# Expert weights fetched four K-rows at a time instead of two, in the same ring of twelve

## The reference, cut to what matters

```
gate = min(h @ w_gate[e] + b_gate[e], 7)
up   = clip(h @ w_up[e] + b_up[e], -7, 7)
y    = ((up + 1) * gate * sigmoid(1.702 * gate)) @ w_down[e] + b_down[e]
```

## Time and profile before

| | |
|---|---|
| median of 3 runs | 1600.43 us (1598.94 to 1605.11) |
| the profiled execution | 1595.97 us |
| its span, first to last instruction | 1594.2 us |
| PE busy | 1525.1 us (96% of the span) |
| DVE busy | 1325.8 us (83%) |
| ACT busy | 1086.6 us (68%) |
| moved by DMA | 464.81 MB, 292 GB/s over the span |
| mean granted TensorE clock | 0.984 of full |

### The profile page before, as it was taken

How to read it: one execution, slowest core, us unless ns; L and a number is a source line. 1 busy time by engine, 2 the same in 40 slices (tenths; PEclk the granted TensorE clock), 3 DMA queues, 4 the chain that set the end, 5 groups by cost and what they waited for, 6 DMA issues and landing times.

```text
span 1594.2 us, 29429 instructions
## 1 busy us (share of the span) xinstructions
PE 1525.1 (96%) x10445; PEld 1262.4 (79%) x10445; DVE 1325.8 (83%) x1458; ACT 1086.6 (68%) x1309; POOL 585.3 (37%) x366
## 2 busy tenths in 40 slices
PE   7999987889999999999999999999999999999993
PEld 6877777886878888878888888888888888888872
DVE  4256455555689999999999999999999999999994
ACT  4245431103468887788888888888878888888881
POOL 7000312101022233344445554544554544545532
PEclk9999999999999999999999999999999999999997
DMA  8321110001399999999999999999999999999974
GB/s 295 91 67 40 40 41 3 4 4 67 134 407 383 389 385 375 390 367 396 381 376 395 394 392 391 391 368 385 393 392 396 385 379 384 389 392 398 384 291 129
DMA packets 81414, 464.81 MB, mean 292 GB/s; under 512 B 11658, under 2 KB 12870, under 8 KB 33216
## 3 DMA queue, kind: packets, MB, share of 16 engines
q1 hardware_dynamic: 71424, 438.68, 69.6%
q0 software_dynamic: 9248, 25.05, 7.1%
q10 hardware_dynamic: 672, 0.07, 0.0%
HBM read 449.16 MB, written 23.66 MB: 297 GB/s over the span
## 4 chain that ended last, share of the span: by engine, by line
PE 86%; DVE 9%; DMA 2%; issue 1%; ACT 1%; DVEq 0%; POOLq 0%; POOL 0%; ACTq 0%; SPq 0%
PE banks L369 71%; PE banks L1779 5%; DVE expert_w_lo L310 4%; PE banks L2042 1%; PE banks L2039 1%; PE banks L1872 1%; PE banks L1856 1%; PE banks L1977 1%; PE banks L2024 1%; DMA x_block<-xn_gate_rows,slot_token 1%; PE banks L1899 1%; DMA xn_gate_rows<-gate_of_expert 1%; PE banks L2051 0%; PE banks L2302 0%; PE banks L2279 0%
## 5 line engine op out<-in xcount | busy, mean ns | idle before, releaser
L310 DVE TENSOR_TENSOR expert_w_lo<-expert_w_raw,expert_w_hi 128x1024 fp32r<-128x1024 f32 x768 | 912.2, 1251 | 24.8 <-ACT expert_w_hi L305 24.4
L305 ACT ACTIVATE expert_w_hi<-expert_w_raw 128x1024 fp32r<-128x1024 f32 x768 | 754.4, 1056 | 30.9 <-DMA expert_w_raw<-in_moe_w_down_dram 28.0
L369 PE MATMUL banks<-expert_w_hi,x_block_T_hi 128*128 128x512 f32 x992 | 388.9, 392 | 0.2 <-DVE expert_w_lo L310 0.2
L369 PE MATMUL banks<-expert_w_lo,x_block_T_hi 128*128 128x512 f32 x992 | 386.5, 390 | 0.0
L369 PE MATMUL banks<-expert_w_hi,x_block_T_lo 128*128 128x512 f32 x992 | 386.2, 389 | 0.0
L717 POOL COPY scatter_gates<-slot_gate 128x1 f32 x26 | 208.7, 8028 | 268.6 <-DMA y_sums<-y_block,scatter_rows 268.6
L369 PE MATMUL banks<-expert_w_hi,h_block_T_hi 128*128 128x512 f32 x544 | 216.0, 397 | 6.4 <-DVE h_block_T_lo L1174 3.4
L369 PEld LDWEIGHTS banks<-expert_w_lo,x_block_T_hi 128*128 128x128 f32 x992 | 186.2, 188 | 38.8
L369 PEld LDWEIGHTS banks<-expert_w_hi,x_block_T_hi 128*128 128x128 f32 x992 | 186.5, 188 | 38.4 <-DVE expert_w_lo L310 0.6
L369 PEld LDWEIGHTS banks<-expert_w_hi,x_block_T_lo 128*128 128x128 f32 x992 | 186.4, 188 | 37.8
L369 PE MATMUL banks<-expert_w_lo,h_block_T_hi 128*128 128x512 f32 x544 | 212.8, 391 | 0.0
(11 more groups left out here) (380 smaller groups left out, 1945.9 us busy)
## 6 DMA issues: line engine op xcount, KB each, us to landing
expert_w_raw<-in_moe_w_gate_dram SPq DMA_DIRECT2D x128, 1024.0 KB, 10.1
expert_w_raw<-in_moe_w_up_dram SPq DMA_DIRECT2D x128, 1024.0 KB, 8.0
expert_w_raw<-in_moe_w_down_dram SPq DMA_DIRECT2D x128, 1024.0 KB, 9.8
w_raw<-in_w_in_dram SPq DMA_DIRECT2D x24, 512.0 KB, 3.8
residual<-in_x_dram SPq DMA_DIRECT2D x8, 512.0 KB, 5.0
w_raw<-in_w_out_dram SPq DMA_DIRECT2D x8, 512.0 KB, 3.6
y_sums<-v_shifted SPq DMA_DIRECT2D x5, 512.0 KB, 8.2
xn_gate_rows<-xn SPq DMA_DIRECT2D x4, 512.0 KB, 4.2
```

The costliest lines, as they stand in the source:

```text
L305: act.activation(self.hi[:, k % self.nhl, 0:width], self.raw[:, k % self.nraw, 0:width], ACT.Copy)\
L310: dve.tensor_tensor(self.lo[:, k % self.nhl, 0:width], self.raw[:, k % self.nraw, 0:width], self.hi[:, k % self.nhl, 0:width].bitcast(F32) ...
L369: last = pe.matmul(o, lhs, rhs, start=start and t == 0, stop=stop and t == 2, skip_group_check=preset)
```

## The change

`PAIR` goes from 2 to 4:

```diff
-        PAIR = 2
+        PAIR = 4
         xring = Ring(raw2, whi2, wlo2, NRAW2, NHL2, MOE0, [len(range(i, MOE0, NRAW)) for i in range(NRAW2 // PAIR)], PAIR)
```

## The result

The changed kernel takes 1631.38 us (median of 4 runs, 1629.80 to 1636.24) against 1602.77 us (4 runs, 1598.94 to 1607.33) before: a ratio of 1.0183, 95% interval 1.0145 to 1.0221, 29 us slower. The forecast was 1633 from 1600.43. The profiled execution took 1632.18 us, 36.2 us more than the one of before.

The account below looks back on a forecast made before the run. PE was taken as the bound, 34.5 us a block. The new loop, 5.5 + 0.1 + 2.4 + 17.7 + 9.9 = 35.6, adds 30 x 1.1 = 33 to 1595.97: 1629, plus 4.5 for the median gives 1633; range 1600 to 1660.

Parts of the forecast that it names:

- The loop: Expert stage, from lo k23 to the next lo k23: 35.6 us a block against PE's 34.5, 1.1 more; chance 0.69.
- Step 1: DVE does k0 to k3 after lo k23, then SP issues k12 to k15: 5.5 us and 0.1 to the issue.
- Steps 2 and 3: Issue of k12 to landing of k20: fixed part 2.4 us, then three transfers with the scatter, 17.7 us.
- the saving by longer pieces: 16 KB pieces instead of 8 KB save 0 to 0.5 us of 18.0 us; the middle, 0.3, was taken.
- fixed part: Time from issue to landing apart from the bytes, into an empty queue: 2.4 us, with 1.4 and 2.6 as ends.
- Step 4: Landing of k20 to k23 releases ACT's hi k20, then DVE works to the end of lo k23: 9.9 us.
- The place where it isn't covered is k8: k8 goes out only with k10, at 1028.2; DMA stands still 1.4 us, 2.0 a block with k12, only 0.7 spare.
- Most of this is covered, since the queue is deep: Later issue (n-9 instead of n-11) and later landing of fours cost little, as three or four transfers are under way.
- How many blocks: Blocks 2 to 31 go through the loop, 30 x 1.1 = 33 us; first blocks no longer, opening and tail nothing.
- A: Rival: no change, PE stays the bound if the fixed part is below about 1.6 us; 1600 us, chance 0.16.
- B: Rival: faster, as larger transfers free DMA time and PE's waits between 440 and 720 shrink; 1595 us, chance 0.04.
- C: Rival: scatter lands more than 1.05 us later, making the gather late; a block takes 36.9, total 1672 us, chance 0.11.

Follow-up runs that it names:

- late hand-back only: Kernel before, still two rows a transfer, but both halves of a four issued only once all four old rows have passed lo: 1602.06 us, ratio 0.9992.
- k12 to k23 in pairs: Changed kernel with k12 to k23 fetched as transfers of two rows, k0 to k11 still in fours: 1605.50 us, ratio 1.0009.
- PAIR = 1: One row (512 KB, pieces of 4 KB) for each transfer, each row handed back by itself: 1605.13 us, ratio 0.9982 to the kernel before.
- 1 MB transfers: Kernel before with late issue of fours and no row used before its whole four landed, still two rows a transfer: 1642.70 us, ratio 1.0239.
- k8 kernel: Changed kernel with only k8 to k11 fetched as two transfers of two rows: 1632.07 us, ratio 1.0180.
- Late landing alone: Kernel before, issues unchanged, but ACT starts no row of a four before both its transfers have landed: 1621.51 us, ratio 1.0107.
- taking the fours apart: Changed kernel with chosen fours as two-row transfers: k20 to k23 1631.55 us, k12 to k15 1621.29, both 1617.82, k12 to k23 1605.50, k8 to k11 1632.07.

## Why the prediction was right, step by step

**What bounds the kernel: right.** PE's 34.5 us a block, with DVE and the DMA engines just below. The three kernels without the loss (late hand-back only, k12 to k23 in pairs, PAIR = 1) come back to it, with 34.50 to 34.56.

**The loop: right in its mechanism, a third of its price too much.** Its steps against the block shown above, time 0 at the end of lo k23 (1015.95, as k8 is issued at 1015.98):

- Step 1, k0 to k3 and the issue: 5.6 us said, 5.5 measured (the second up transfer goes out at 1015.98 + 5.84 - 0.33 = 1021.5).
- Steps 2 and 3, issue of k12 to the landing of k20: 2.4 + 17.7 = 20.1 said, 1021.5 to 1041.2 = 19.7 measured. The one term with a size of its own here is the saving by longer pieces: 0.3 was taken as the middle of 0 to 0.5. Against 1 MB transfers it is 0.43 a block between two kernels, so the runs support at most 0.13 of the 0.4. With 17.6 to 17.8 for the three transfers and the scatter (18.0 less the 0.43, or less half of it, since the three are half of a block's transfers), 1.9 to 2.1 is left for the fixed part where 2.4 was taken; no run measures that part by itself, and whether it or the scatter holds the rest isn't settled.
- Step 4, landing of k20 to lo k23: 9.9 said, 1041.2 to 1051.2 = 10.0 measured (k8 of the next block goes out at 1051.22). Inside it lo k20 took 1.85 us in place of 1.21 and the hidden rows 1.23 in place of 1.77: POOL's spread of the gate bias ran beside the hidden rows before (1020.38, for 1.30 us) and runs beside lo k20 now (1041.36, for 1.90).
- Sum: 35.6 said, 35.24 by the rows and 35.29 on average measured. The mechanism held and the term was 0.3 to 0.4 too large, a third of the 1.1 a block.
- The estimate by the Trainium skill ("DMA: Bandwidth & Descriptors", section "Anatomy of one DMA"), a loop of 35.2, came nearer to the measured 35.24. But the page fits its 2.0 us to DMAs issued from GpSimd, and these go out on SP's queue, so the agreement isn't shown to be more than chance.
- Two slips in the working: the two rates behind the 0.3 give a constant of 5.4% at 8 KB, and the 2.7% is half of it; and the 2.4 stands for transfers of 512 KB, not for the size of these.

**"The place where it isn't covered is k8": wrong as a cause.** The k8 kernel shows that nothing hangs on it. In the sum it did no harm, since step 2 already let k12 decide.

**"Most of this is covered, since the queue is deep": too kind to the late landing.** The prediction charged it at k20 alone. Late landing alone costs 17 us, and 0.78 us in a steady block, and taking the fours apart showed three landings (k12, k16, k20) that DVE waits for, in loops of nearly the same length. The late issue, on which the prediction laid the weight, costs only in company. So the loop that was summed is one of three of about the same length, and cutting it alone won nothing: its length was right, but the prediction took it for the only bound.

**How many blocks: the step that was off the other way.** The prediction took the first blocks' loop as no longer. The first seven distances of `up_act` (the first start at 473.5 and 476.1, the eighth at 708.9 and 726.3) are 235.4 us before and 250.2 after: 2.1 a block in place of 1.1. The 24 distances behind them (to 1537.2 and 1575.0) bring 20.4, the opening 2.6, and the tail gives 1.6 back: 36.2. (Over all kernels here the opening ends between 472.3 and 485.6 in the profiled executions, without regard to their loss, so its 2.6 says nothing.) So the total came out near 33 by luck: a steady term that was too high met an early one that was too low.

Which waits make the early loss isn't settled block by block. One candidate in the timelines explains little of it. At its first spread of a gate bias POOL stands still for reasons of its own ("issue"), before and after:

```profile
536.89 1.85 POOL L725 PARTITION_BROADCAST gate_bias_rows<-gate_bias_rows  x1 [11.31 <-issue]
```
```profile
545.09 1.30 POOL L725 PARTITION_BROADCAST gate_bias_rows<-gate_bias_rows  x1 [16.57 <-issue]
```

By `up_act` this block takes 40.3 us after (537.97 to 578.24) and 36.8 before (532.27 to 569.08), and ACT waits 5.65 us for that spread where it waited 1.51. But with PAIR = 1, which loses nothing, ACT waits 3.8 us there and the block takes 39.4. For what POOL waits is not shown. The three kernels without the loss need 238.8 to 240.5 us for the seven distances, and so does late landing alone (240.3); the changed kernel needs 250.2, with 1 MB transfers 254.9. So some 10 of the 14.8 us come from late landing and late hand-back together, in the fours of k12 to k23, and the other 5 are no more than kernels without the loss differ among themselves.

**The rivals.** A asked for a fixed part below about 1.6 us (1.3 to 1.5 by its own sum); the 1.9 to 2.1 that is left above is longer, if the scatter takes its 3.2 us. The block of 35.29 is what decides against A. B: nothing was faster, and PAIR = 1 shows that there was little to win. C: the scatter lands some 10 us after its issue as before (POOL waits 10.33 us at L717 in this block, 10.87 in the earlier trace rows), so it was not delayed. The rule of the Trainium skill to batch ("DMA: Bandwidth & Descriptors", section "Bandwidth") asks for at least 1 MiB, which the kernel before already had. Its table gives larger transfers a larger share of the peak, for DMAs issued from GpSimd, and the transfers here agree in direction (0.43 us a block for 2 MB against 1 MB, measured). The kernel got slower all the same, since it needed its rows early more than it needed them cheaply.

**What it should show.** DMA share 3 to 6% below 1: 0.96, right. PE 96 to 98 of 100: 97.75 in the named stretch, but over 800 to 1500 it is 693.83 of 700, 99.1. A block is 0.78 us longer, 2.2% of it, but the profile books 0.5 of that as busy PE (34.98 us a block); the weight loads (PEld) show the waits, 23.1 us for `lo` in that stretch, where they had none before. The chain through DVE and the transfers: right. ACT's landing waits at k12, k16 and k20, several times 28 us: right, 107.5. Issues to landing of 7 (up) to 11 us (down): 7.3 for k8 and 10.1 for k16.

## What to carry to other kernels

Of a ring of fixed size, a larger transfer takes away twice: its rows come later and its slots go out later. Look for the landing that a nearly full engine waits for, not for the mean depth of the queue: a landing that cost nothing before, or 0.46 us of ACT's time, is then the bound, and an engine with 97% of work can't make it up. Where several groups are tight to the same degree, taking one apart shows nothing; try them together before the theory is given up, and keep the large transfers for the rows that have time.

## What the runs showed of the hardware

- Transfers of 2 MB with pieces of 16 KB are cheaper for their bytes than transfers of 1 MB with pieces of 8 KB: 0.43 us a block (12.6 MB). The packets themselves take 309 ns for 8 KB before and 611 ns for 16 KB after (medians of the trace's records), 7 ns less for 16 KB. Each of the 16 DMA engines moves 48 such pieces a block, so by an estimate 0.34 us of its time a block is saved by the longer piece. From 8 down to 4 KB the DMA share in 800 to 1500 rises from 1.01 to 1.03 at the same 388 GB/s, and the time doesn't change.
- When POOL spreads a bias row over the partitions, one DVE instruction beside it is stretched: a subtraction of 1.21 us takes 1.7 to 2.2 us, or the hidden rows 1.77 in place of 1.23. That happened at 54 of 58 spreads before and at 56 of 58 in the changed kernel, and the subtractions next to it kept their 1.21. Which instruction is hit moves with the landing of the bias.
- Single disturbed blocks: the changed kernel has one of 37.3 us among its steady ones (a transfer of k12 took 11.8 us instead of 9.7 to land, at 1056.72). The kernel before has none in its 24. More bytes in flight are not shown to be the reason: both edits with 1 MB transfers, where landings are waited for too, have none either. Why that transfer was slow is open.
